# Attention scores from rounded halves: three single-pass products in place of one plain fp32 product

## What is computed

```python
q = (u @ w_q).reshape(bsz, S, N_DIFF_HEADS, 2, DIFF_HEAD_DIM)
scale = DIFF_HEAD_DIM ** -0.5
qb = lax.dynamic_slice_in_dim(q, start, Q_BLOCK, axis=1)
logits = jnp.einsum("bqhcd,bkhcd->bhcqk", qb, k).astype(jnp.float32) * scale
logits = logits + bias.astype(jnp.float32)[None, :, None]
logits = jnp.where((dist >= 0)[None, None, None], logits, -jnp.inf)
p = jax.nn.softmax(logits, axis=-1)
attn = p[:, :, 0] - lam * p[:, :, 1]
return jnp.einsum("bhqk,bkhe->bqhe", attn.astype(v.dtype), v)
```

## Time and profile before

| | before |
|---|---|
| median of 3 runs | 2521.91 (2521.76 to 2521.96) |
| the profiled execution's own time | 2523.18 |
| span of the profile | 2521.2 |
| PE busy | 2506.2 (99%) |
| VectorE busy | 1822.3 (72%) |
| ScalarE busy | 1247.9 (49%) |
| mean DMA rate | 188 GB/s |

### The profile page before, as it was taken

The page is one execution under the profiler, slowest core; times in us unless marked ns, Lnnn a source line. Parts: engine busy times, 40 slices in busy tenths (PEclk is TensorE's granted clock), DMA queues, the critical chain, the costliest instruction groups (busy, mean ns, idle before and its releaser), DMA issues.

```text
span 2521.2 us, 42149 instructions
## 1 busy us (share of the span) xinstructions
PE 2506.2 (99%) x15444; PEld 2238.8 (89%) x15444; DVE 1822.3 (72%) x2572; ACT 1247.9 (49%) x1631; POOL 155.6 (6%) x271
## 2 busy tenths in 40 slices
PE   8999999999999999999999999999999999999999
PEld 8999999999898888888888998998898888888887
DVE  6977877787876675766667876778866667576667
ACT  7555555554654444444444754455644444444444
POOL 2222112211100000000000000000000000000000
PEclk9999999999999999999999999999999999999999
DMA  7666556656566566666656555555566656666664
GB/s 216 212 199 199 175 184 192 206 166 196 172 190 193 183 197 189 191 191 190 192 183 198 194 176 176 179 173 168 184 189 188 192 183 198 190 191 192 190 192 151
DMA packets 267240, 474.10 MB, mean 188 GB/s; under 512 B 16673, under 2 KB 50066, under 8 KB 265618
## 3 DMA queue, kind: packets, MB, share of 16 engines
q1 hardware_dynamic: 264194, 457.53, 59.2%
q0 software_dynamic: 2624, 15.00, 1.7%
q10 hardware_dynamic: 336, 0.41, 0.0%
HBM read 470.70 MB, written 2.19 MB: 188 GB/s over the span
## 4 chain that ended last, share of the span: by engine, by line
PE 98%; DVE 1%; ACT 1%; DMA 0%; issue 0%; SPq 0%; ACTq 0%; DVEq 0%
PE ps L1615 23%; PE ps L1616 23%; PE ps L1617 23%; PE ps L1644 16%; PE ps L1646 9%; PE ps L1873 1%; PE ps L1751 0%; PE ps L1971 0%; DMA h<-x 0%; PE ps L1878 0%; PE ps L1810 0%; PE ps L1779 0%; PE ps L2001 0%; PE ps L1729 0%; PE ps L1735 0%
## 5 line engine op out<-in xcount | busy, mean ns | idle before, releaser
L993 DVE TENSOR_TENSOR whl<-raw,whl 128x1024 fp32r<-128x1024 f32 x856 | 1062.5, 1242 | 592.1 <-ACT whl L664 579.5
L664 ACT ACTIVATE whl<-raw 128x1024 fp32r<-128x1024 f32 x856 | 906.7, 1059 | 1086.8 <-PE ps L1617 735.9
L1644 PE MATMUL ps<-xhl,whl 128*128 128x512 f32 x1792 | 623.0, 391 | 0.0
L1646 PE MATMUL ps<-xhl,whl 128*128 128x256 f32 x1792 | 505.4, 282 | 0.0
L1615 PE MATMUL ps<-whl,bhl 128*128 128x512 f32 x1284 | 500.8, 390 | 0.0
L1616 PE MATMUL ps<-whl,bhl 128*128 128x512 f32 x1284 | 499.5, 389 | 0.0
L1617 PE MATMUL ps<-whl,bhl 128*128 128x512 f32 x1284 | 499.5, 389 | 0.0
L1615 PE MATMUL ps<-xhl,whl 128*128 128x256 f32 x1748 | 493.9, 283 | 0.0
L1616 PE MATMUL ps<-xhl,whl 128*128 128x256 f32 x1748 | 488.5, 279 | 0.0
L1617 PE MATMUL ps<-xhl,whl 128*128 128x256 f32 x1748 | 487.9, 279 | 0.0
L1644 PEld LDWEIGHTS ps<-xhl,whl 128*128 128x128 f32 x1792 | 336.4, 188 | 70.9
(11 more groups left out here) (268 smaller groups left out, 2084.6 us busy)
## 6 DMA issues: line engine op xcount, KB each, us to landing
raw<-mlp_w SPq DMA_DIRECT2D x512, 512.0 KB, 4.2
raw<-a_in_proj SPq DMA_DIRECT2D x161, 512.0 KB, 4.5
raw<-a_out_proj SPq DMA_DIRECT2D x64, 512.0 KB, 4.0
raw<-b_w_q SPq DMA_DIRECT2D x32, 512.0 KB, 4.0
raw<-w_k SPq DMA_DIRECT2D x32, 512.0 KB, 4.0
raw<-w_v SPq DMA_DIRECT2D x32, 512.0 KB, 3.6
raw<-b_out_proj SPq DMA_DIRECT2D x32, 512.0 KB, 3.7
cumb<-cum_scratch POOLq DMA_DIRECT2D x8, 1024.0 KB, 7.7
```

The source lines that it names most:

```text
L664: sc.activation(slot_of(s, lo)[0], raw_of(s), ACT.Copy).then_inc(hi_ready, 1)
L993: ve.tensor_tensor(out=low, in0=raw_of(s), in1=hi.bitcast(F32), op=ALU.subtract).then_inc(lo_ready, 1)
L1644: te.matmul(ps[:, f, :].rearrange("p (q n) -> p q n", q=2), wh[:, j, c], xboth[:, :, k, :], start=k == 0, stop=False, skip_group_check=True)
L1646: last = te.matmul(ps[:, f, 0:S], wl[:, j, c], xhi[:, k, :], start=False, stop=k == KT - 1, skip_group_check=True)
```

## The change

Both q and k are kept as two fp32r halves: `qth`, `qtl`, `kth` and `ktl`. The scaled k goes first to the buffer `ob`; ScalarE rounds it into `kth`, VectorE subtracts to get `ktl`. ScalarE's copy of q now writes the rounded half, and VectorE subtracts it from PSUM. Each of the four products of a head becomes three single-pass ones, and in the program the two components alternate. The plans move `made`, `logits` and `weigh` of heads 0 and 1 by one slab, and PE's wait for q and k moves from v1 to v2. `kth` and `ktl` lie where `postw` (a norm weight) lies, so one load of `postw` moves from the start of the attention layer to behind the last scores.

```diff
-USUAL_PLAN = Plan((-7, -7, 0, 0), (0, 1, 0, 1), (-7, -4, 0, 2), (-5, -2, 4, 6), (3, 5, 7, 9), (5, 7, 9, 11), (7, 9, 11, 13),
+USUAL_PLAN = Plan((-6, -6, 0, 0), (0, 1, 0, 1), (-6, -3, 0, 2), (-4, -1, 4, 6), (3, 5, 7, 9), (5, 7, 9, 11), (7, 9, 11, 13),
                   5, 6, (7, 2, 7, 2))
-LAST_PLAN = Plan((-7, -7, 0, 2), (0, 1, 0, 0), (-7, -4, 0, 2), (-5, -2, 4, 6), (3, 5, 7, 9), (5, 7, 9, 11), (7, 9, 11, 13),
+LAST_PLAN = Plan((-6, -6, 0, 2), (0, 1, 0, 0), (-6, -3, 0, 2), (-4, -1, 4, 6), (3, 5, 7, 9), (5, 7, 9, 11), (7, 9, 11, 13),
                   0, 1, (7, 2, 7, 2))
...
-        postw = sb("postw", [P, D])
+        first_use = ExitStack()
+        postw = sb("postw", [P, D], F32, first_use)
+        first_use.close()
+        k_room = sb("k_room", [P, D], F32R)
...
-        qt = mb("qt", [P, HG, S])
-        kt_ = mb("kt", [P, HG, S])
+        qth, qtl = mb("qth", [P, HG, S], F32R), mb("qtl", [P, HG, S], F32R)
+        kth, ktl = (k_room[:, i * HG * S:(i + 1) * HG * S].rearrange("p (f s) -> p f s", f=HG) for i in range(2))
...
+        k_scaled = ob[:, :, :, :].rearrange("p f c n -> p f (c n)")
...
-            next_postw(2, w["norm_post_mix"][1])
...
+            pool.wait_ge(lg_ready, HG * QG)
+            next_postw(2, w["norm_post_mix"][1])
             next_postw(3, w["norm_post_mlp"][1])
...
                 if (unit, i) == ("k", 7 if first else 0):
-                    sc.activation(qt[:, :, :].rearrange("p f s -> p (f s)"), ps[:, 0:2, :].rearrange("p b n -> p (b n)"),
-                                  ACT.Copy).then_inc(q_copied, 1)
+                    sc.activation(qth[:, :, :].rearrange("p f s -> p (f s)"), ps[:, 0:2, :].rearrange("p b n -> p (b n)"),
+                                  ACT.Copy).then_inc(q_hi, 1)
+                if (unit, i) == ("v", 0):
+                    act.wait_ge(k_whole, g + 1)
+                    sc.activation(kth, k_scaled, ACT.Copy).then_inc(k_hi, 1)
...
-                    ve.tensor_tensor(out=kt_[:, :, :], in0=ps[:, 3:5, :].rearrange("p b (f s) -> p (b f) s", f=2),
-                                     in1=rs_row[:, :].unsqueeze(1).to_broadcast([P, HG, S]), op=ALU.mult).then_inc(k_copied, 1)
+                    ve.tensor_tensor(out=k_scaled, in0=ps[:, 3:5, :].rearrange("p b (f s) -> p (b f) s", f=2),
+                                     in1=rs_row[:, :].unsqueeze(1).to_broadcast([P, HG, S]), op=ALU.mult).then_inc(k_whole, 1)
+                if (unit, i) == ("k", 7 if first else 0):
+                    dve.wait_ge(q_hi, g + 1)
+                    ve.tensor_tensor(out=qtl[:, :, :].rearrange("p f s -> p (f s)"), in0=ps[:, 0:2, :].rearrange("p b n -> p (b n)"),
+                                     in1=qth[:, :, :].rearrange("p f s -> p (f s)").bitcast(F32), op=ALU.subtract).then_inc(q_copied, 1)
+                if (unit, i) == ("v", 0):
+                    dve.wait_ge(k_hi, g + 1)
+                    ve.tensor_tensor(out=ktl, in0=k_scaled, in1=kth.bitcast(F32), op=ALU.subtract).then_inc(k_copied, 1)
...
-                        for c in range(2):
-                            cs = slice(c * DH, (c + 1) * DH)
-                            te.matmul(ps[:, pair[c], 0:S], qt[cs, i, P:], kt_[cs, i, :], start=True, stop=True,
-                                      skip_group_check=True)
-                            last = te.matmul(ps[:, pair[c], S:S + P], qt[cs, i, 0:P], kt_[cs, i, 0:P], start=True,
-                                             stop=True, skip_group_check=True)
+                        for rows, keys, cols in ((slice(P, S), S, slice(0, S)), (slice(0, P), P, slice(S, S + P))):
+                            for n_term, (q, k) in enumerate(((qth, kth), (qth, ktl), (qtl, kth))):
+                                for c in range(2):
+                                    cs = slice(c * DH, (c + 1) * DH)
+                                    last = te.matmul(ps[:, pair[c], cols], q[cs, i, rows], k[cs, i, 0:keys],
+                                                     start=n_term == 0 and keys == S, stop=n_term == 2, skip_group_check=True)
                         last.then_inc(lg_done, 1)
...
-                    if i == 1:
+                    if i == 2:
                         pe.wait_ge(q_copied, g + 1)
                         pe.wait_ge(k_copied, g + 1)
```

More of the change, by code:

```diff
@@ L411, in build @@
         q_copied, k_copied, v_copied = sem("q_copied"), sem("k_copied"), sem("v_copied")
+        q_hi, k_whole, k_hi = sem("q_hi"), sem("k_whole"), sem("k_hi")
         lg_done, lg_ready, ex_ready, at_ready, at_t, at_copied = (
```

## The result

The changed kernel took 2526.51 us (median of 20 executions, 2525.10 to 2527.95), the kernel before in the same rounds 2521.92 (20 executions, 2521.73 to 2522.96). The ratio is 1.0018, 95% interval 1.0011 to 1.0024: 4.6 us slower, within the 0.2% (5.0 us) that the prediction called no change. I had forecast 2524.4, with 2521.2 to 2530.5 as the range.

What follows compares the result with a forecast made beforehand. PE, busy 384.12 of the attention stage's 385 us, bounds the kernel. Products -0.2 and waits +2.75 give +2.5: 2525.7 against the profiled execution, 2524.4 against the median 1.27 lower; range 2521.2 to 2530.5.

Steps and rivals of the forecast that it cites:

- The waits: PE's waits for ScalarE's copy of v behind q0: 1.65 us more in group 1, 1.1 in group 3, sum +2.75.
- PE does not wait for k behind v2: Group 0: VectorE finishes k's remainder at 1463.1, PE needs it at 1463.4; hidden by 0.3 us.
- nothing stands before out0 and out1: Groups 1 and 3: no idle time of PE before the first product of either output slab; 0.2 us left.
- the components overlap: Score products: a head's two components, alternating in program order, run side by side, 0.675 us per head.
- short products: Rival: fp32r products of 128 columns stream four times, 0.213 us each; +5.0, 2529.4 us; chance 0.14.
- components in turn: Rival: alternating components do not overlap, a head is 1.35 us; +10.8, 2535.2 us; chance 0.10.
- loads that do not bind: Rival: 128-key products cost only their stream, 0.054 us, a head 0.52; -2.6, 2521.8 us; chance 0.05.
- waits that do not grow: Rival: VectorE or ScalarE make up the slab, so PE waits no longer; 2521.7 us; chance 0.07.
- The moved load of `postw`: Behind the last scores, 6.5 us to land, about twenty slabs of 2.7 before the norm reads it: costs nothing.
- The products: Score visits on PE for 16 heads: 14.9 us before, 14.7 after, a gain of 0.2.
- The term of the late load: Visits to two heads: a late weight load of 0.11 us at the second head goes when components alternate.
- the fall in the longer wait: PE's granted clock falling during the longer wait: named as a way to be wrong, with no term.

Runs made afterwards that it cites:

- late-wait version: The changed kernel with PE's wait for the copy of v moved from q0 to q2; 2522.36 us, ratio 1.0002.
- alternating plain run: The kernel before, with PE's wait for v moved from q0 to q2 and the two components' plain products alternating; 2520.16 us, ratio 0.9994.
- one-by-one run: The changed kernel with PE's wait for v at q2 and each head's 12 products sorted by component; 2524.12 us, ratio 1.0009.

## Why the prediction came out as it did

**What was right.** The waits, the larger part of the sum: +1.65 at q0 of group 1, measured 1.63 (+1.1 at q0 of group 3, measured 1.08; 1.63 and 1.15 in the run with the shift alone). The mechanism, one v slab of delay less one slab copy, is seen in ScalarE's rows, and the late-wait version removes it. PE does not wait for k behind v2, since k's remainder is done half a microsecond before the slab's last product starts; nothing stands before out0 and out1; the components overlap, though the earlier trace rows, from which this was argued, are products on two halves of the array's columns and not of its rows; the load binds at 128 keys nearly as at 256. Thus the rivals of short products (0.21 each), of components in turn (1.35 a head), of loads that do not bind and of waits that do not grow are all denied. The moved load of `postw` costs nothing in any trace, as forecast.

**What was off in size.** The products: I had -0.2, and the nine visits gave -0.6 by their own lengths. The term of the late load, 0.11 per second head, was right (0.10 in the alternating plain run). A second head, 0.675 by my sum, adds 0.69. A first head with its switching, 1.10 by my sum, costs 1.04: the sum has no term for the pair of 128 keys that starts after 0.06 in place of 0.11. A part of this gain is not seen in the time, because PE waits for `ob` behind it.

**What had no term.** First, the clock. I had named the fall in the longer wait as a way to be wrong, but gave it neither a price nor a chance, though the wait that I forecast was 2.4 us long. In the profiled execution it costs 2.8; over the executions it makes the median 1.4 higher than with the wait filled (2526.51 against 2525.07). Second, VectorE's backlog: the step "their work is free as long as nothing that PE waits for comes late" was followed for the copies of k and v but not for `ob`. I looked at 87 us of idle time in the stage as one sum, while at the end of group 3 there is none. It is +1.15 from `out2` on, of which the run with the shift alone has 0.85 and the wait for `h` makes the rest.

With these, from the median: 2521.9 + 1.6 + 1.1 - 0.6 + 1.2 = 2525.2, which is what the five executions with a clock of 1.000 show (2525.15), and 1.4 more for the clock gives 2526.6, the median. The forecast was 2.1 us low. That the result still lies in the stated range is in part luck: the range reached up to 2530.5 for the sake of the short products, which did not come, and left room for two costs that had no term.

**What stays open.** Why the slower executions of the changed kernel lie mostly 1.5 and seldom 2.8 above the others: only one trace of a fall was taken. Where the lateness that VectorE and ScalarE hand to each other in `out1` begins: it comes with the shift and is seen in the exponentials' waits of 1.35 and 0.79, but I have not followed it back to one step, and no run removes it. What the pause of VectorE before `h` comes from. What the halves cost without any shift of the plan was not tried.

## What to carry to other kernels

Splitting an fp32 product into three single-pass ones saves nothing where every product brings its own weight load and half of the products are short. At 128 and 256 columns the load sets a pace of about 0.115 us. An estimate from these paces and the earlier trace rows: three products make 0.35, where a plain one of 256 columns makes 0.43 and one of 128 columns 0.21, so what the long products gain goes to the short ones; measured, the visits came out even (1.84 against 1.83). The order of products on different rows of the array is worth more, and costs nothing: alternate them. When a step is moved a slab later, follow it to each of its readers, price the wait on PE with the clock that may fall behind it, and ask whether the engine that must catch up has idle time left at that very place, not in the stage as a whole.

## What the hardware showed unexpectedly

- A stand-still of PE of 2.3 us was enough to lower the granted clock, and not always. In the profiled execution of the changed kernel it fell from 1.00 to 0.50 after 1.9 us without work and stayed there for 6.8 us; in that of the shift alone it stayed at 1.00 through a stand-still of 2.35. By their mean clock, 15 of 20 executions of the one and 5 of 11 of the other were below 1.000. Behind the wait of 1.08 in group 3 the clock stayed at 1.00.
- Products on different rows of the array are not started in the order of the program: in the one-by-one run component 1 began 0.28 us ahead of the last product of component 0, which stands before it. The Trainium skill (TensorE: Matmul & The Clock Gate, The mechanism) says that matmuls start and end strictly in program order; the starts in this trace do not agree, and its ends are modelled and tell nothing. The figure of the same page of the Trainium skill (Why this matters for your kernels) for tiles on different rows, at most 4 ns from start to start, agrees with the 3 to 4 ns of most pairs of single-pass products here; the pairs of plain products start 6 to 14 ns apart.
- Doubling the columns of a product from 128 to 256 cost 0.015 us each in the visits to two heads, where 128 more columns stream for 0.054: the weight load was already the longer part.
